# A chunked RWKV layer on one core: the output chain kept in PSUM, and the first inverse factor made by VectorE's 32x32 block transposition

## The reference

```
def step(state, inp):
    r_t, w_t, k_t, v_t, a_t, b_t = inp
    sa = jnp.einsum('bhvk,bhk->bhv', state, a_t)
    state = (state * w_t[:, :, None, :] + sa[..., None] * b_t[:, :, None, :]
             + v_t[..., None] * k_t[:, :, None, :])
    return state, jnp.einsum('bhvk,bhk->bhv', state, r_t)
...
mean = jnp.mean(y, axis=-1, keepdims=True)
var = jnp.mean(jnp.square(y - mean), axis=-1, keepdims=True)
y = ((y - mean) * lax.rsqrt(var + GN_EPS)).reshape(B, S, RW_DIM) * gn_w + gn_b
bonus = jnp.sum(rh * kh * r_k.astype(jnp.float32), axis=-1, keepdims=True) * vh
out = (y + bonus.reshape(B, S, RW_DIM)) * g
```

## Time and profile before

| what | value |
|---|---|
| median of the runs | 4068.55 us |
| the profiled execution: its own time, its span | 4068.22 us, 4066.2 us |
| busy over the span: PE, PEld, DVE | 3872.5, 3168.5, 1986.2 us |
| busy over the span: ACT, POOL | 1635.8, 1658.2 us |
| granted TensorE clock, mean | 0.975 |

### The profile page before, as it was taken

How to read it: one execution, slowest core, us unless ns; L and a number is a source line. 1 busy time by engine, 2 the same in 40 slices (tenths; PEclk the granted TensorE clock), 3 DMA queues, 4 the chain that set the end, 5 groups by cost and what they waited for, 6 DMA issues and landing times. The chain is left out here.

```text
span 4066.2 us, 67108 instructions
## 1 busy us (share of the span) xinstructions
PE 3872.5 (95%) x28244; PEld 3168.5 (78%) x28244; DVE 1986.2 (49%) x3042; ACT 1635.8 (40%) x2723; POOL 1658.2 (41%) x902
## 2 busy tenths in 40 slices
PE   8999988999999899998899999989999999999998
PEld 6888867878887788886787888777878887787887
DVE  7778674236534777777413654436141123523112
ACT  5554434343334554543434433446232224523222
POOL 4444412434445444441243444534444444444443
PEclk9999999989999899999998999989999999999999
DMA  3111113225532211111232554221322322122222
GB/s 134 47 44 48 50 61 107 99 93 193 186 136 99 87 43 44 49 54 63 102 104 84 196 189 137 99 73 42 104 86 96 99 93 78 52 91 91 99 98 83
DMA packets 108730, 379.52 MB, mean 93 GB/s; under 512 B 12560, under 2 KB 12944, under 8 KB 107792
## 3 DMA queue, kind: packets, MB, share of 16 engines
q1 hardware_dynamic: 98208, 357.27, 25.9%
q10 hardware_dynamic: 10224, 17.97, 1.2%
HBM read 359.46 MB, written 15.73 MB: 92 GB/s over the span
## 5 line engine op out<-in xcount | busy, mean ns | idle before, releaser
L293 POOL TENSOR_TENSOR Wlo<-raw,Whi 128x1024 fp32r<-128x1024 f32 x552 | 1339.2, 2429 | 2002.0 <-ACT Whi L280 2001.8
L228 PE MATMUL ps<-hh,Whi 128*128 128x512 f32 x2864 | 1151.9, 402 | 28.4 <-DVE hl L377 10.1
L228 PE MATMUL ps<-hh,Wlo 128*128 128x512 f32 x2864 | 1123.2, 392 | 0.0
L228 PE MATMUL ps<-hl,Whi 128*128 128x512 f32 x2864 | 1123.0, 392 | 0.0
L280 ACT ACTIVATE Whi<-raw 128x1024 fp32r<-128x1024 f32 x552 | 581.8, 1055 | 705.2 <-PE ps L228 601.3
L228 PEld LDWEIGHTS ps<-hh,Whi 128*128 128x128 f32 x2864 | 542.7, 189 | 160.4 <-issue 28.2
L228 PEld LDWEIGHTS ps<-hl,Whi 128*128 128x128 f32 x2864 | 543.1, 190 | 117.0 <-issue 8.6
L228 PEld LDWEIGHTS ps<-hh,Wlo 128*128 128x128 f32 x2864 | 542.1, 189 | 115.8
L228 PE MATMUL ps<-gh,Whi 128*128 128x512 f32 x864 | 337.5, 391 | 3.8 <-POOL Wlo L293 3.8
L228 PE MATMUL ps<-gh,Wlo 128*128 128x512 f32 x864 | 336.2, 389 | 0.0
L228 PE MATMUL ps<-gl,Whi 128*128 128x512 f32 x864 | 336.2, 389 | 0.0
(11 more groups left out here) (363 smaller groups left out, 5947.3 us busy)
## 6 DMA issues: line engine op xcount, KB each, us to landing
raw<-in_stream SPq DMA_DIRECT2D x554, 512.0 KB, 3.5
ada<-in_ada SPq DMA_DIRECT2D x96, 512.0 KB, 4.5
park_x<-xT SPq DMA_DIRECT2D x2, 2048.0 KB, 7.3
park_yh<-yh ACTq DMA_DIRECT2D x16, 256.0 KB, 2.1
park_yl<-yl ACTq DMA_DIRECT2D x16, 256.0 KB, 2.3
xT<-park_x SPq DMA_DIRECT2D x2, 2048.0 KB, 8.7
yrh<-park_yh ACTq DMA_DIRECT2D x16, 256.0 KB, 8.4
yrl<-park_yl ACTq DMA_DIRECT2D x16, 256.0 KB, 8.6
```

The costliest lines, as they stand in the source:

```text
L228: last = pe.matmul(ps, left[a](k), right[c](k), start=start and k == 0 and i == 0, stop=stop and k == n - 1 and i == 2)
L293: pool.tensor_tensor(b["Wlo"][:, slot], b["raw"][:, raw_slot(b, u)], b["Whi"][:, slot].bitcast(F32), SUB) \
```

## The change

Three things are edited. First, level 0's X no longer goes through TensorE and ScalarE: VectorE adds the identity to the masked matrix for all 128 partitions into `Wc` and transposes it in 32x32 blocks into `X`. Second, the six output operations of a pair write and read the PSUM bank that the reciprocal deviation came in, in place of the SBUF tile `dd` (an alias of `y`). Third, VectorE's mixing of r for the next pair stands behind the level-0 work instead of ahead of it. Two waits follow: the bank counts as free after the low part (`yl`), and GpSimd's mask of level 2 waits for VectorE's X in place of TensorE's product.

```
 def rwkv_inv_pe(pe, s, b, p, amid, between):
-    for h in range(2):
-        pe.wait_ge(s["inv_v"], INV_V(p, f"T0{h}"))
-        for c in range(BLK):
-            for u in range(2):
-                last = pe.matmul(b["ps"][half(1 - u), 4 + h, block(c)], b["XT"][half(u), h, block(c)], b["c"]("identc")[half(u)],
-                                 start=True, stop=True)
-        last.then_inc(s["inv_p"], 1)
     for l in range(1, LEVELS):
         for h in range(2):
             pe.wait_ge(s["inv_g"], INV_G(p, f"m{l}{h}"))
-            if l > 1:
-                pe.wait_ge(s["inv_v"], INV_V(p, f"X{l - 1}{h}"))
-            else:
-                pe.wait_ge(s["inv_a"], INV_A(p, f"X0{h}"))
+            pe.wait_ge(s["inv_v"], INV_V(p, f"X{l - 1}{h}"))
...
 def rwkv_inv_act(act, s, b, p, between):
-    for h in range(2):
-        act.wait_ge(s["inv_p"], INV_P(p, f"X0{h}"))
-        act.activation(b["X"][:, h], b["ps"][:, 4 + h, 0:BLK * CB], ACT.Copy).then_inc(s["inv_a"], 1)
...
 def rwkv_inv_dve(dve, s, b, p, between):
...
+        dve.tensor_tensor(blocks(b["Wc"][:, h]), blocks(b["TM"][:, h, 0]), ident, ADD).then_inc(s["inv_v"], 1)
+    for h in range(2):
+        dve.wait_ge(s["inv_v"], INV_V(p, f"i{h}"))
+        dve.transpose(b["X"][:, h], b["Wc"][:, h]).then_inc(s["inv_v"], 1)
     between(0)
...
 def rwkv_out_dve(dve, s, b, p):
...
-    dve.tensor_tensor(b["dd"], b["dd"], rwkv_bank(b, "post", p, "rr"), MUL).then_inc(s["post_v"], 1)
+    ps = rwkv_bank(b, "post", p, "rr")
+    dve.tensor_tensor(ps, b["dd"], ps, MUL).then_inc(s["post_v"], 1)
     done("yn")
-    dve.tensor_scalar(b["dd"], b["dd"], b["p"]("gnw", p), b["p"]("gnb", p), MUL, ADD).then_inc(s["post_v"], 1)
+    dve.tensor_scalar(ps, ps, b["p"]("gnw", p), b["p"]("gnb", p), MUL, ADD).then_inc(s["post_v"], 1)
     done("ya")
-    dve.tensor_tensor(b["dd"], b["dd"], b["rk"][:, p % 2], ADD).then_inc(s["post_v"], 1)
+    dve.tensor_tensor(ps, ps, b["rk"][:, p % 2], ADD).then_inc(s["post_v"], 1)
...
-    dve.tensor_tensor(b["dd"], b["dd"], b["gS"][:, p % 3], MUL).then_inc(s["post_v"], 1)
+    dve.tensor_tensor(ps, ps, b["gS"][:, p % 3], MUL).then_inc(s["post_v"], 1)
...
-    dve.tensor_copy(b["yh"][:], b["dd"]).then_inc(s["post_v"], 1)
+    dve.tensor_copy(b["yh"][:], ps).then_inc(s["post_v"], 1)
...
-    dve.tensor_tensor(b["yl"][:], b["dd"], b["yh"][:].bitcast(F32), SUB).then_inc(s["post_v"], 1)
+    dve.tensor_tensor(b["yl"][:], ps, b["yh"][:].bitcast(F32), SUB).then_inc(s["post_v"], 1)
...
         rwkv_front_dve(dve, s, b, p)
-        if p + 1 < PAIRS:
-            rwkv_mix_dve(dve, s, b, p + 1, "r")
...
                 if l == 0:
-                    rwkv_mix_dve(dve, s, b, p + 1, "k")
+                    rwkv_mix_dve(dve, s, b, p + 1, "rk")
                     rwkv_scan_dve(dve, s, b, p + 1)
```

More of the change, by code:

```diff
@@ L449 @@
 INV_G = Steps("m00", "m01", *[f"m{l}{h}" for l in range(1, LEVELS) for h in range(2)])
-INV_P = Steps("X00", "X01", *[f"{m}{l}{h}" for l in range(1, LEVELS) for m, h in
+INV_P = Steps(*[f"{m}{l}{h}" for l in range(1, LEVELS) for m, h in
                               (("W", 0), ("W", 1), ("X", 0), ("T", 0), ("X", 1), ("T", 1))
                               if not (m == "X" and l == LEVELS - 1)])
-INV_A = Steps("d00", "d01", "d10", "d11", "X00", "X01", *[f"W{l}{h}" for l in range(1, LEVELS) for h in range(2)])
-INV_V = Steps("t00", "T00", "t01", "T01", *[f"{m}{l}{h}" for l in range(1, LEVELS) for h in range(2) for m in "XT"
+INV_A = Steps("d00", "d01", "d10", "d11", *[f"W{l}{h}" for l in range(1, LEVELS) for h in range(2)])
+INV_V = Steps("t00", "T00", "i0", "t01", "T01", "i1", "X00", "X01", *[f"{m}{l}{h}" for l in range(1, LEVELS) for h in range(2) for m in "XT"
                               if not (m == "X" and l == LEVELS - 1)])
@@ L548, in freed_count @@
         return s["post_a"], POST_A(p, "sd")
-    return s["post_v"], POST_V(p, {"bonus": "bv", "mean": "d", "rr": "yn"}[x])
+    return s["post_v"], POST_V(p, {"bonus": "bv", "mean": "d", "rr": "yl"}[x])
 def rwkv_bank(b, *key):
@@ L1105, in rwkv_inv_pool @@
                 if l >= 2:
-                    pool.wait_ge(s["inv_p"], INV_P(p, f"W{l - 2}{h}") if l > 2 else INV_P(p, f"X0{h}"))
+                    pool.wait_ge(*((s["inv_p"], INV_P(p, f"W{l - 2}{h}")) if l > 2 else (s["inv_v"], INV_V(p, f"X0{h}"))))
             pool.tensor_tensor(blocks(b["TM"][:, h, l % 2]), blocks(b["TD"][:, h]), lvl[:, l].broadcast_to([P, BLK, CB]), MUL)                 .then_inc(s["inv_g"], 1)
@@ L1494, in attention_pe @@
         if i == 9:
-            pe.wait_ge(s["post_v"], POST_V(PAIRS - 1, "yn"))
+            pe.wait_ge(s["post_v"], POST_V(PAIRS - 1, "yl"))
         split_matmuls(pe, b["ps"][:, i % 4], columns_of(w, KD), h, KD).then_inc(s["qkv_p"], 1)
```

## The result

The changed kernel takes 4084.11 us (median of 5 runs, 4081.32 to 4089.58) where the kernel before takes 4068.55 (4067.92 to 4072.67): a ratio of 1.0037, with a 95% interval of 1.0025 to 1.0050. Forecast were 4039.0 us and a range of 4029 to 4054. The profiled execution took 4083.65 us, with a span of 4081.8, 15.6 more than the span before.

The account below looks back on a forecast made before the run. TensorE was taken to bound the time mix, busy 54.67 of 55.85 us a pair. Removing level-0 products (17.0 us) and the wait for `M` (12.5) saves 29.5 us, giving 4039.0 us, range 4029 to 4054 for 8 in 10.

Parts of the forecast that it names:

- The level-0 products go: Start of the inverse on TensorE: level 1 starts 1.26 us earlier in 14 pairs, 17.0 us net of pair 7's loss.
- X in time: VectorE's X before level 1: transpositions 0.42 us each, cover 1.8 to 4.3 us in pairs 0 to 6, late in pair 7.
- The race with the weight part: VectorE's last level-0 addition against GpSimd's weight part: if lost, it ends at about 423.6 instead of 421.2.
- The output chain: Six VectorE operations in PSUM: 4.3 us instead of 7.03, removing TensorE's wait at line 819, 12.5 us gained.
- The moved mixing and the added work: VectorE ahead of level 1's updates: r mixing moved, two additions and two transpositions added, costed at nothing with 1.7 us cover.
- the changed waits come earlier than before: ScalarE and GpSimd released earlier: no cost booked; other small waits might go too, giving the range's lower end of 4030.
- The slower one: Rival at level 0: dear transpositions, 2.5 us each, delay level 1 and its updates, 3 us in 16 pairs; 4104 us, chance 0.07.
- The clock: TensorE's clock: fewer gaps might bring one more stretch at 1.2 GHz, costing half its length; it only widens the range.
- The 4039.0 us: Whole kernel with both gains: forecast median time, own range 4030 to 4047, chance 0.70.

Follow-up runs that it names:

- chain_only: The kernel before with only the output chain moved to PSUM, level 0 and the r mixing left as before: 4055.99 us, ratio 0.9969.
- turn_xt: The changed kernel with X made by four 64-partition transpositions of XT, without the two additions into `Wc`: 4078.89 us, ratio 1.0023 to the kernel before.
- bonus_first: The changed kernel with only VectorE's bonus operation put ahead of the preparation behind the level 1 updates: 4068.58 us, ratio 0.9996 to the kernel before.
- kkr_early: The changed kernel with bonus, then running sum behind level 1 updates, kkr right behind r and k mixing, ScalarE awaiting cum only before its exponentials: 4039.48 us.

## Why the prediction was wrong, step by step

- **The level-0 products go: right, to the tenth.** The distance from line 711 to level 1 fell from 2.34 to 1.08 us in all of the 14 pairs 0 to 6, as forecast, and rose to 2.55 in pair 7. With level 1 of pair 7 later by 0.26 us (behind Y of pair 6), where 0.3 was forecast, that is some 17 us.
- **X in time: right.** A transposition takes 0.395 to 0.439 us where 0.42 was taken. The race with the weight part was lost in all 14 (2.60 to 2.64 us), as the text allowed, and X was in time in pairs 0 to 6.
- **The output chain: right.** Five of the six operations take 0.69 to 0.70 us and gain and bias 0.82; the gate takes 0.70 in all 16 where its median was 2.73. chain_only gives 13.5 us where 12.5 were forecast; in the changed kernel's trace it is 14.6 less 1.8. The lock rule of the Trainium skill ("SBUF — State Buffer", "Who interferes with whom") fits this, and turn_xt's 0.44 us transpositions beside a weight part too. Its advice against many operations in PSUM ("VectorE: DVE Perf Modes", "Rules for kernel authors") is right on the single operation (gain and bias 0.82 against 0.55 at best), and wrong here on the sum.
- **The moved mixing and the added work: this step failed.** It said "I cost the move at nothing; the cover is about 1.7 us", and reached 428.7 for the end of the running sum, 3.0 us behind level 1, by adding undisturbed durations: 2 x 1.4 and 1.37. Measured are 6.31 us. The mixing took 3.9 us (428.77 to 432.69) and the running sum 4.0. (The section on the change counts ten operations between the masking and the running sum; there are twelve, in place of eight.) The term that was put at nothing measures 47.8 us between level 1 and product, the clock's some 7 included. I had counted the first weight part's collision and dropped the second, because I had it meet cm as before; but once VectorE was late the operation in its way was the running sum, which stands ahead of the updates. It also said "On ScalarE and GpSimd the changed waits come earlier than before" and booked that as harmless, at the lower end of the range even as a gain. The masks released early lie beside the mixing; undoing only that gave 11 us.
- **The second deadline was not seen at all.** The text asked when the updates are wanted at level 2 (0.7 to 0.8 us late) and not when the bonus is. With 21.8 us in 12 pairs it is the larger wait, and bonus_first shows that it can be bought off alone.
- **The rivals.** The slower one had the right place (VectorE's work behind level 0 pushes the level 1 updates past TensorE's demand), but hung on a dear transposition, so it got 0.07. Its 3 us a pair were also too many by its own numbers: with level 1 at 428.0, level 2 asks for the updates at 434.1, so the "about 2 us behind" counts the late start twice; that the pairs did lose some 3 us each is luck. The cover of 1.7 us was less than one collision of 2.1 us, and that should have been a rival by itself. The clock stood there with "fewer gaps" as its reason; it fell behind waits, new and longer ones.
- **The 4039.0 us.** kkr_early takes 4039.48, so both gains are there in full; but it needs two reorderings that the prediction did not have, and is no confirmation of its reading of the queue.

## What to carry to other kernels

When an edit fills up the idle time ahead of a result that the busiest engine wants, recount the queue with collisions, not with undisturbed durations: list what GpSimd will be doing in the new order, and take every operation with two SBUF inputs in its way as long as GpSimd's longest one (here 2.6 us). Ask of an earlier release which work it puts beside which. And before counting work as moved for nothing, look up every wait that ends in that queue; here the fix was to put the two wanted results ahead of the preparation, to make kkr early for ScalarE, and to keep the change, which makes 4084 into 4039 us.

## What was not expected of the hardware

The lower clock came with modest idle times: stretches of 3.4 us at 1.2 GHz stand in four pairs of layer 2 of the changed kernel, each about 1.7 us dear, in a stage where TensorE is busy for 53.7 of 56.4 us. The same waits of 0.74 and 1.82 us stand in layer 1 without them, so which pair is hit was not settled. And a tenth of a microsecond decides which of the two engines pays. The `Wc` addition that started at 425.53, 0.05 us behind the weight part at 425.48, took 2.62 us in place of 0.43. In the kernel before, a mixing operation of the same kind started 0.11 us ahead of a weight part: it took 0.68 us, and the weight part 2.82 in place of about 2.4.

```profile
1378.58 0.68 DVE L980 TENSOR_TENSOR dz<-zp 128x512 f32<-128x512 f32 x1
```
```profile
1378.69 2.82 POOL L293 TENSOR_TENSOR Wlo<-raw,Whi 128x1024 fp32r<-128x1024 f32 x1 [0.58 <-ACT Whi L280]
```
